# Mamba-2 decays in a hybrid decoder layer: the cumulated sums go to all partitions by a DRAM round trip instead of selecting matmuls

## The reference

```
dt = softplus(dt_raw + dt_bias);  A = -exp(A_log)
a = dt * A                               # per token and head, never positive
a_cs = cumsum(a, over tokens)
decay_in = exp(where(l >= s, a_cs[l] - a_cs[s], -inf))   # per head, 256 x 256
CB = einsum('lgn,sgn->gls', C, B)                        # per group
y_diag = (CB * decay_in) @ (X * dt)                      # per head, 256 x 64
```

## Time and profile before

| | us |
|---|---|
| runs without profile | 558.83, 558.90, 559.13 (median 558.9) |
| profiled execution | 558.88 |
| its span, first to last instruction | 557.1 |
| PE busy | 542.9 (97%) |
| DVE busy | 436.1 (78%) |
| ACT busy | 333.2 (60%) |
| POOL busy | 63.9 (11%) |

### The profile page before, as it was taken

One profiled execution on the slowest core, in us unless ns is written; L12 is line 12 of the kernel. 1 busy time (PEld: TensorE's weight loads), 2 busy tenths in 40 slices (PEclk: granted clock), 3 DMA queues, 4 the chain that ended last, 5 costly groups with the idle time before them and its releaser, 6 DMA issues.

```text
span 557.1 us, 9770 instructions
## 1 busy us (share of the span) xinstructions
PE 542.9 (97%) x3670; PEld 494.9 (89%) x3670; DVE 436.1 (78%) x659; ACT 333.2 (60%) x539; POOL 63.9 (11%) x97
## 2 busy tenths in 40 slices
PE   8999999999999989999999999999999999999994
PEld 5999899999999879998889678889999999999993
DVE  4899898888887884877766666589898988888845
ACT  6757566555654565857675874376566556556533
POOL 2003000000000420512431002000000000000015
PEclk9999999999999999999999999999999999999998
DMA  9867955545664357555324235345575566655302
GB/s 269 291 227 233 322 190 189 167 175 186 226 226 151 91 158 229 167 188 176 128 78 151 75 82 167 131 154 169 198 251 201 178 208 226 226 161 182 108 1 75
DMA packets 69359, 97.65 MB, mean 175 GB/s; under 512 B 1862, under 2 KB 55298, under 8 KB 69331
## 3 DMA queue, kind: packets, MB, share of 16 engines
q1 hardware_dynamic: 68336, 94.55, 52.1%
q0 software_dynamic: 848, 2.47, 1.5%
q10 hardware_dynamic: 146, 0.27, 0.1%
HBM read 96.23 MB, written 1.05 MB: 175 GB/s over the span
## 4 chain that ended last, share of the span: by engine, by line
PE 81%; DVE 8%; ACT 3%; DMA 3%; issue 2%; POOL 1%; SPq 0%; POOLq 0%; DVEq 0%; ACTq 0%
PE bank L1575 25%; PE bank L1577 25%; PE bank L1576 25%; DMA raw<-in_ffn_w 3%; DVE w_lo L1048 2%; PE bank L1716 1%; ACT decay L924 1%; DVE x L1065 1%; ACT w_hi L602 1%; POOL rstd L472 1%; PE bank L1881 1%; PE bank L1882 1%; PE bank L1868 1%; DVE normed L1457 1%; PE bank L1880 0%
## 5 line engine op out<-in xcount | busy, mean ns | idle before, releaser
L1575 PE MATMUL bank<-hT_hi,w_hi 128*128 128x256 f32 x736 | 208.7, 284 | 0.2 <-DVE tok_rows L1216 0.2
L1576 PE MATMUL bank<-hT_lo,w_hi 128*128 128x256 f32 x736 | 208.0, 283 | 0.0
L1577 PE MATMUL bank<-hT_hi,w_lo 128*128 128x256 f32 x736 | 208.0, 283 | 0.0
L1048 DVE TENSOR_TENSOR w_lo<-raw,w_hi 128x1024 fp32r<-128x1024 f32 x128 | 158.4, 1240 | 28.5 <-ACT w_hi L602 28.0
L602 ACT ACTIVATE w_hi<-raw 128x1024 fp32r<-128x1024 f32 x128 | 134.1, 1055 | 43.4 <-PE bank L1577 24.7
L1575 PEld LDWEIGHTS bank<-hT_hi,w_hi 128*128 128x128 f32 x736 | 140.8, 191 | 3.3 <-DVE tok_rows L1216 1.4
L1576 PEld LDWEIGHTS bank<-hT_lo,w_hi 128*128 128x128 f32 x736 | 140.8, 191 | 1.6
L1577 PEld LDWEIGHTS bank<-hT_hi,w_lo 128*128 128x128 f32 x736 | 140.9, 191 | 0.0
L1575 PE MATMUL bank<-w_hi,hT_hi 128*128 128x512 f32 (+1 forms) x192 | 70.1, 365 | 2.0 <-DVE w_lo L1082 1.0
L1577 PE MATMUL bank<-w_hi,hT_lo 128*128 128x512 f32 (+1 forms) x192 | 68.1, 355 | 0.0
L1576 PE MATMUL bank<-w_lo,hT_hi 128*128 128x512 f32 (+1 forms) x192 | 68.0, 354 | 0.0
(11 more groups left out here) (217 smaller groups left out, 810.4 us busy)
## 6 DMA issues: line engine op xcount, KB each, us to landing
raw<-in_ffn_w SPq DMA_DIRECT2D x54, 1024.0 KB, 5.4
raw<-in_w_in SPq DMA_DIRECT2D x16, 1024.0 KB, 5.5
tok_rows<-in_ffn_w SPq DMA_DIRECT2D x10, 1024.0 KB, 5.3
raw<-in_w_out SPq DMA_DIRECT2D x6, 1024.0 KB, 4.9
raw<-in_ffn_w SPq DMA_DIRECT2D x8, 256.0 KB, 5.3
x<-in_x SPq DMA_DIRECT2D x4, 256.0 KB, 3.9
out_x<-normed SPq DMA_DIRECT2D x3, 256.0 KB, 2.3
norm_w<-in_mix_norm POOLq DMA_DIRECT2D x1, 512.0 KB, 5.4
```

What stands on the lines that cost most here:

```text
L1048: dve.tensor_tensor(lo, src, hi, ALU.subtract).then_inc(half_ready, 1)
L1575: pe.matmul(dst, lhs[0], rhs[0], start=start, stop=False, skip_group_check=True)
L1576: pe.matmul(dst, lhs[0], rhs[1], start=False, stop=False, skip_group_check=True)
L1577: return pe.matmul(dst, lhs[1], rhs[0], start=False, stop=stop, skip_group_check=True)
```

## The change

The selecting and the masking matmuls are dropped. `csT` is now a plain float32 tile of 16 rows of 256. POOL stores it into a DRAM tensor `cs_heads` (16 KB), waits until it has landed, and loads it back in three DMAs that repeat it on all 128 partitions: heads 0 to 7 (1 MB) into `norm_w`, heads 8 to 11 (0.5 MB) into a part of `normed`, heads 12 to 15 (0.5 MB) into a part of `z_silu`. `cs_row(h)` names the place of a head's row. ACT's `decay_exp` now serves two heads at a time: four Relu activations form max(own sum - row's sum, 0) in `decay`, then one Exp of 384 columns for each head, with scale -1, in place. The Relu makes the entries above the diagonal of a diagonal block 0, hence their decay 1; so POOL multiplies the two diagonal blocks of each group's C.B by the triangle of ones first (`cb_mask`). The loads of the two later norms' weights into `norm_w` move behind the rotation of k. Core of the diff:

```
+            def cb_mask():
+                for g in range(GROUPS):
+                    pool.wait_ge(cb_ready, g + 1)
+                    own = cb[:, g, :].rearrange("p (j c) -> p j c", c=P)[:, 0:3:2, :]
+                    pool.tensor_tensor(own, own, tri[:, 0:P].unsqueeze(1).to_broadcast([P, 2, P]), ALU.mult).then_inc(cb_masked, 1)
+            def cs_spread():
+                pool.wait_ge(csT_ready, 1)
+                pool.dma_start(cs_heads, csT[:, :]).then_inc(cs_stored, 16)
+                pool.wait_ge(scaled_right, 4)
+                pool.wait_ge(transposed, 8)
+                pool.wait_ge(sq_ready, sq_count(1, 1) + 2)
+                pool.wait_ge(cs_stored, 16)
+                for j, place in enumerate((norm_w[:, :, :], normed[:, :, 0:512], z_silu[:, :, 512:1024])):
+                    h = (0, 8, 12)[j]
+                    src = cs_heads[h:h + (8, 4, 4)[j], :].rearrange("(t a) l -> t (a l)", t=TT)
+                    pool.dma_start(place, src.partition_broadcast(P)).then_inc(cs_loaded[j], 16)
...
-            pool.dma_start(norm_w[:, 0, :], norms[2].partition_broadcast(P)).then_inc(norm_loaded[2], 16)
-            pool.wait_ge(scaled_right, 4)
-            pool.dma_start(norm_w[:, 1, :], norms[3].partition_broadcast(P)).then_inc(norm_loaded[3], 16)
             softplus()
-
-            pool.wait_ge(transposed, 8)
+            cb_mask()
+            cs_spread()
...
             rotate(k_tok)
+            for j in range(2):
+                pool.wait_ge(decay_ready, 4 * (j + 1))
+                pool.dma_start(norm_w[:, j, :], norms[2 + j].partition_broadcast(P)).then_inc(norm_loaded[2 + j], 16)
...
-            act.wait_ge(consts_loaded, 16)
-            act.activation(ident_r[:, :], ident, ACT.Copy).then_inc(consts_r, 1)
-            act.activation(mask_r[:, :], cst[:, C_MASK:C_MASK + P], ACT.Copy).then_inc(consts_r, 1)
-            act.activation(select_r[:, :], cst[:, C_SEL:C_SEL + SH], ACT.Copy).then_inc(consts_r, 1)
...
-            def decay_exp(h):
-                act.wait_ge(bc_done, h + 1)
-                if h >= 2:
-                    act.wait_ge(m_ready, 2 * (h - 1))
-                for s, (a, b) in enumerate(((0, 256), (256, 384))):
-                    act.activation(decay[:, h % 2, a:b], bank[:, 4 + h % 2, a:b], ACT.Exp,
-                                   bias=dts[:, 7, s, h:h + 1]).then_inc(decay_ready, 1)
+            def decay_exp(h0):
+                if h0 in (0, 8, 12):
+                    act.wait_ge(cs_loaded[h0 // 4 - 1 if h0 else 0], 16)
+                for h in (h0, h0 + 1):
+                    if h >= 2:
+                        act.wait_ge(m_ready, 2 * (h - 1))
+                    for s, (a, b) in enumerate(((0, 256), (256, 384))):
+                        act.activation(decay[:, h % 2, a:b], cs_row(h)[:, s * P:], ACT.Relu,
+                                       bias=dts[:, 7, s, h:h + 1], scale=-1.0).then_inc(decay_arg, 1)
+                for h in (h0, h0 + 1):
+                    act.wait_ge(decay_arg, 2 * (h + 1))
+                    act.activation(decay[:, h % 2, :], decay[:, h % 2, :], ACT.Exp, scale=-1.0).then_inc(decay_ready, 1)
...
             def cumsum_T_out():
                 dve.wait_ge(csT_done, 1)
-                step(dve.tensor_copy(csT[:, :], bank[:, 7, 0:384]))
-                lo = slice(2 * SH, 3 * SH)
-                dve.tensor_tensor(csT[lo, :], bank[lo, 7, 0:384], csT[lo, :].bitcast(f32),
-                                  ALU.subtract).then_inc(csT_ready, 1)
+                dve.tensor_copy(csT[:, :], bank[0:SH, 7, 0:SEQ]).then_inc(csT_ready, 1)
...
                 if 20 <= m < 28:
-                    for h in (2 * (m - 20), 2 * (m - 20) + 1):
-                        ssd_out(h)
-                        if h + 2 < SH:
-                            decay_args(h + 2)
+                    ssd_out(2 * (m - 20))
+                    ssd_out(2 * (m - 20) + 1)
```

More of the change, by code:

```diff
@@ L65 @@
 GU_BANK = 3
-C_ID, C_TRI, C_MASK, C_COS, C_SIN, C_SEL, C_AHEAD, C_END = 0, 128, 384, 512, 544, 576, 592, 848
+C_ID, C_TRI, C_COS, C_SIN, C_SEL, C_AHEAD, C_END = 0, 128, 384, 416, 448, 464, 720
 LEAST = -3.0e38
@@ L83, in shape_constants @@
     c[:, C_TRI + P:C_TRI + 2 * P] = 1.0
-    c[:, C_MASK:C_MASK + P] = np.where(np.triu(np.ones((P, P))) > 0, 0.0, MASKED)
     inv = (np.float32(THETA) ** (-np.arange(0, ROT, 2, dtype=np.float32) / np.float32(ROT))).astype(np.float32)
@@ L146, in build @@
         dts = sb("dts", [P, 8, TT, SH])
-        csT = sb("csT", [P, 384], f32r)
+        csT = sb("csT", [SH, SEQ])
+        cs_heads = nc.dram_tensor("cs_heads", (SH, SEQ), f32, kind="Internal").ap()
         cb = sb("cb", [P, GROUPS, 384])
@@ L274, in build @@
         csT_ready = sem("csT_ready")
+        cs_stored = sem("cs_stored")
+        cs_loaded = [sem(f"cs_loaded{j}") for j in range(3)]
         tap_ready = sem("tap_ready")
@@ L279, in build @@
         cb_ready = sem("cb_ready")
+        cb_masked = sem("cb_masked")
         xT_done = sem("xT_done")
@@ L283, in build @@
         proj_out = sem("proj_out")
-        bc_done = sem("bc_done")
+        decay_arg = sem("decay_arg")
         decay_ready = sem("decay_ready")
@@ L301, in build, with cs_row @@
         block = ctx.enter_context(nc.Block())
+        def cs_row(h):
+            if h < 8:
+                return norm_w[:, h // 4, (h % 4) * SEQ:(h % 4 + 1) * SEQ]
+            t, c = h % 4 // 2, h % 2 * SEQ
+            return normed[:, t, c:c + SEQ] if h < 12 else z_silu[:, t, 512 + c:512 + c + SEQ]
         def cols_half(t, half):
@@ L1378, in _ @@
             mix_lo(5)
-            v, ncs = (dts[:, j, :, :] for j in (0, 7))
+            v = dts[:, 0, :, :]
             def softplus_argument():
@@ L1399, in cumsum_out @@
                 dve.tensor_copy(cs_rows[:, :, 0:SH], cs).then_inc(cs_tok_ready, 1)
-                dve.tensor_copy(cs_rows[:, :, 2 * SH:3 * SH], cs).then_inc(cs_tok_ready, 1)
-                dve.wait_ge(cs_tok_ready, 2)
-                step(dve.tensor_scalar(ncs, cs_rows[:, :, 0:SH], -1.0, None, ALU.mult))
+                dve.tensor_copy(dts[:, 7, :, :], cs).then_inc(cs_tok_ready, 1)
             def cumsum_T_out():
                 dve.wait_ge(csT_done, 1)
-                step(dve.tensor_copy(csT[:, :], bank[:, 7, 0:384]))
-                lo = slice(2 * SH, 3 * SH)
-                dve.tensor_tensor(csT[lo, :], bank[lo, 7, 0:384], csT[lo, :].bitcast(f32),
-                                  ALU.subtract).then_inc(csT_ready, 1)
+                dve.tensor_copy(csT[:, :], bank[0:SH, 7, 0:SEQ]).then_inc(csT_ready, 1)
             def conv_taps(j0):
@@ L1434, in weigh @@
                 if h == 0:
-                    dve.wait_ge(cb_ready, 2)
+                    dve.wait_ge(cb_masked, 2)
                 if h >= 2:
                     dve.wait_ge(y_done, h - 1)
+                dve.wait_ge(decay_ready, h + 1)
                 for s, (a, b) in enumerate(((0, 256), (256, 384))):
-                    dve.wait_ge(decay_ready, 2 * h + s + 1)
                     dve.scalar_tensor_tensor(mix_m[:, h % 2, a:b], cb[:, g, a:b], dts[:, 6, s, h:h + 1],
@@ L1786, in cumsum_T @@
                 pe.wait_ge(cs_tok_ready, 2)
-                for j, t in enumerate((0, 1, 1)):
-                    last = pe.transpose(bank[:, 7, j * P:(j + 1) * P], cs_rows[:, t, :], ident)
+                for t in range(TT):
+                    last = pe.transpose(bank[:, 7, tok(t)], cs_rows[:, t, :], ident)
                 last.then_inc(csT_done, 1)
@@ L1850, in chunk_half @@
                 chunk_part(m, 1).then_inc(half_used, 1)
[L1852 to L1871, removed]
             def ssd_out(h):
@@ L1994, in _ @@
                     x_transposes(1)
-                if m == 19:
-                    decay_args(0)
-                    decay_args(1)
                 if 20 <= m < 28:
-                    for h in (2 * (m - 20), 2 * (m - 20) + 1):
-                        ssd_out(h)
-                        if h + 2 < SH:
-                            decay_args(h + 2)
+                    ssd_out(2 * (m - 20))
+                    ssd_out(2 * (m - 20) + 1)
                 if m == 22:
@@ L2007, in _ @@
                 if m == 27:
-                    mix_transposes(0, D_ATTN, decay_ready, 2 * SH)
+                    mix_transposes(0, D_ATTN, cb_ready, 2)
                 if 29 <= m < 32:
```

5 lines of the change are left out of this document (removed).

## The result

The changed kernel takes 562.11 us (median of 6 runs, 561.09 to 562.88), the kernel before beside it on the same chip 559.18 (558.83 to 559.67). The ratio is 1.0054, with a 95% interval of 1.0044 to 1.0065: 2.9 us slower. The forecast was 2.6 faster. The profiled execution took 562.33 us with a span of 560.4, 3.3 more than before.

What follows compares the result with a forecast made beforehand. PE was taken as the bound, busy 542.9 of 557.1 us. Its saving of 5.2 less costs of 0.3, 1.0 and 1.3 gave -2.6, so 556.3 us from 558.9, range 554.6 to 559.2.

Steps and rivals of the forecast that it cites:

- What leaves PE: PE, halves 20 to 28: dropped decay matmuls and one transpose of the sums take 5.2 us off the path.
- What comes onto ACT: ACT, per pair of heads: four Relus 1.38 us, two Exps in a row 0.45 each; 2.3 against 1.3 before.
- The start: Half 20, heads 0 and 1: PE waits behind ACT's Relus, table load and Exp; 1.0 us lost.
- the 0.3 for ACT's extra work: Halves with other ACT work: 4.4 us against PE's 4.0, mostly covered; 0.3 charged, bounds 0 and 1.0.
- The middle: m = 24 and 25: DVE's line is fixed, so PE waits at heads 10 and 11; loss 1.3, bounds 0.8 and 1.8.
- The DRAM copy: Sums' round trip ahead of head 0: store 4.0, 1 MB copy 6.4, landed at 262.9, wanted at 263.5; cost 0.
- The value taken costs nothing: First copy's landing at 262.9 is ahead of ACT's need at 263.5, so no cost; the upper end costs 2.8.
- The upper end: Latest landing allowed for the first 1 MB copy: 266.3, a cost of 2.8 us.
- rival B: First copy lands between 264 and 266.2; gain shrinks to between 2.1 and 0, 556.8 to 558.9; chance 0.15.
- The price of lateness: ACT's wait for the first copy: past 263.5 each microsecond of delay is a microsecond of the end.
- C: Rival: first copy lands after 266.1, head 0 late by more than PE saves; 560.8 for 268; chance 0.10.
- D: Rival: gain given back later, in the attention part, where up to 2 us go; 558.3; chance 0.08.

Runs made afterwards that it cites:

- run 6: Changed kernel with SP holding the weight load of 258.04 until the 1 MB copy has landed: 555.63 us, ratio 0.9932.
- run 7: run 4 with the gate of the first eight heads moved on DVE behind heads 10 and 11: 554.53 us, ratio 0.9905.
- run 2: Changed kernel with 18 small unused matmuls on PE between half 20 and head 0: 560.21 us, ratio 1.0013.
- Run 8: Changed kernel with the cumulated sums transposed and copied to SBUF one half earlier, POOL still issuing the DMAs: 555.84 us, ratio 0.9931.
- run 4: Changed kernel with store and three copies issued by SP, behind the weight load of unit 12, instead of by POOL: 555.64 us, ratio 0.9926.
- run 9: Changed kernel with SP issuing store and copies, sums transposed one half earlier, gate behind heads 10 and 11: 554.59 us, ratio 0.9923.
- run 10: run 9 with a four-element Exp on ACT, so the table load stands ahead of the copies of x_tok: 553.49 us, ratio 0.99.
- run 1: Changed kernel without the round trip: copies read same-size rows of input x, issued right behind the masking: 556.14 us, ratio 0.9935.
- run 5: Changed kernel with POOL issuing the second and third copy only when the first decay is there: 562.73 us, ratio 1.0061.

## Why the prediction was wrong, step by step

**What leaves PE, 5.2 us.** Right. In run 6 the eight pairs of heads take 10.9 us on PE instead of 14.9, with 0.6 of waiting in them, and the 0.57 ahead of half 20 is gone: 5.1.

**What comes onto ACT.** Right in size: four Relus took 1.49 (taken 1.38, within the bounds of 1.2 and 1.6), two Exps 0.94 (taken 0.97).

**The start, 1.0, and the 0.3 for ACT's extra work.** Somewhat too high. Counted as the prediction counts it, from the handover of the matmul before, head 0 in run 6 is 0.45 late (266.56 + 0.23, and it starts at 267.24). The second pair is 0.52 longer than a pair without a wait (1.80, against 1.28). That is 1.0 against 1.3.

**The middle, 1.3.** Somewhat too high. Head 10 is 1.26 late in run 6, where it was 0.34 late before, and head 11 by 0.1: 1.0 more. It goes when the gate is moved (run 7).

**A term that the sum lacks, 0.4.** A half behind a pair of heads takes 2.85 (268.60 to 271.45 in run 6); behind `decay_args` it took 2.75 (269.72 to 272.47 in the kernel before). Over the eight halves that makes 0.4.

Together that is -5.1 + 1.0 + 1.0 + 0.4 = -2.7 for the stretch with the copy in time, as measured, and the forecast was -2.6. It is so close partly by luck: 0.6 too much in two terms stands against 0.4 in a term that was not seen.

**The DRAM copy, 0.** This is the step that failed, by both of its terms. The store was taken as 4.0 (landed at 256.5) and took 5.2 (257.9). The 1 MB copy was taken as 6.4, with a bound of 9.0, and took 9.1. "The value taken costs nothing" was therefore wrong: landed at 267.5 where ACT wanted it at 263.3. What was missed in both terms is what was issued just ahead of them. The prediction did not see that the store has the load of 252.07 ahead of it. For the copy it saw the weight load begin to move at 259 and let it share from there; it did not see that the load would be issued 0.4 us before the copy, so that 2 MB move before the copy has landed. The first miss makes the second: with a store of 4.0 and the same 0.5 of handing over, the copy would have gone out at about 257.2 (an estimate from these rows), ahead of the load of 258.04. The upper end took 4.8 and 9.0, close to what was measured, but the values taken lay well below, and rival B had it that both being slow is unlikely. They were not independent; loads just ahead made both slow.

**The price of lateness** was right: "each microsecond of delay is a microsecond of the end". 267.5 - 263.5 = 4.0, and 556.3 + 4.0 = 560.3; run 2, in which PE keeps its clock, measured 560.2. The rate is what the runs show (4.5 us for 4.4 of ACT's waiting, run 2 against 6); that the totals meet to 0.1 is luck, since the kernel with the copy in time is 0.7 faster than 556.3 and the wait 0.4 longer than 4.0.

**The clock** stood in no step. A wait of 4.6 us on PE was followed by 1.2 GHz until 277.5. Head 0 to head 2 took 6.96 us instead of 4.20 (run 2); 0.6 of these 2.8 come back: behind the stretch at the low level PE no longer waits for DVE at the second pair, which takes 1.25 instead of run 2's 1.82. What stays is 2.0 in the stretch of the table, 1.9 by the medians.

**The rivals.** C was the mechanism, with 0.10: landing at 268 was put at 560.8, which is 560.3 for the 267.5 at which it landed; the difference to 562.1 is the clock. C asked for a store of 6 and a copy of 9.5; 5.2 and 9.1 with 0.7 of handing over did it. D fell: the row at 304.00 before is 3.65 later, the first of the attention part as much (311.38 against 307.72), and the span is 3.3 longer, so behind the stretch nothing is lost and 0.35 comes back. The upper end of 266.3 for the landing was short by 1.2: 0.4 of the store, 0.1 of the copy, and 0.7 of handing over (the store left 0.2 and the copy 0.5 later than the landing or the sums ahead of it allowed in the sum).

The Trainium skill was drawn on for the 2.0 us of a DMA's fixed cost ("DMA: Bandwidth & Descriptors", Anatomy of one DMA). Run 8 agrees with it for a store that has nothing ahead of it (1.8 us). The 1 MB copy alone took 4.3 to 4.9 us, up to 0.5 from the 4.4 that the prediction worked out as an estimate from this section of the Trainium skill. For the store behind a load another section bears: in "Queues, rings and completion order" the same page of the Trainium skill says that a DMA's semaphore lands only after every earlier write of the same DMA engine, across its queues. The traces agree: in the changed kernel and in runs 4 and 6 the 16 KB store landed 0.1 to 0.2 us after the 1 MB load issued 0.4 to 0.6 us ahead of it, from POOL's queue as from SP's. That this rule is the mechanism, and not the load's packets on the way, no run here shows.

## What to carry to other kernels

Before a small DMA is put on the path of waits, look at what has been issued just ahead of it and not yet landed, in any queue: here a 16 KB store cost 1.8 us or 5.2, and a 1 MB copy 4.9 or 9.1, by whether a weight load stood ahead of them. In a chain of DMAs ask too whether a late first one pushes the second behind a load. A prefetch that nobody needs for a long time can be held by one wait, and that was worth 6.5 us. And a wait on PE as long as the one here should be priced twice, as time (4.5) and as the low clock behind it (2.0). When two executions differ elsewhere by a microsecond, compare the stretch that the edit touches, and not the spans.

## What the runs showed of the hardware

- A 16 KB store issued 0.4 to 0.6 us behind a 1 MB load landed just after that load, from another queue as from the same: 4.9 to 5.2 us from POOL, 5.1 to 5.3 from SP. It took 1.8 with nothing in flight and the load 0.9 us behind it.
- The load ahead was not slowed by the 1 MB copy that another queue issued 0.4 us behind it (5.5 us, changed kernel), while the copy took 9.1.
- An idle time of 4.6 us on PE was followed by a granted clock of 0.50, to 5.8 us after work had begun again; with one of 0.78 us (run 2) it stayed at 1.00.
- The 1 MB copy to 128 partitions took 4.3 to 4.9 us with no load in flight ahead of it (runs 4, 6, 7, 9, 10), 6.8 and 6.9 with one issued 1.2 and 1.5 us ahead (runs 1 and 8), and 8.8 to 9.4 with one issued 0.3 to 0.4 us ahead (changed kernel, runs 2 and 5). No run has a load in another queue right behind the copy, so how much is the order and how much the sharing is not shown apart.
